# Hybrid encoder block: five weight slots in the down phase, its ring loads on SyncE, weight sums two blocks behind

## The reference

```python
gate, val = jnp.split(u @ w_up[i], 2, axis=-1)
gate = causal_depthwise_conv(gate, ffn_dw_w[i], ffn_dw_b[i])
f = (jax.nn.gelu(gate, approximate=True) * val) @ w_down[i]     # the down phase
h = h + rms_norm(f, g_post_ffn[i])
h = h + (p[i] @ w_ple[i]) * jax.nn.sigmoid(h @ w_ple_gate[i])
```

## Time and profile before

| | us |
|---|---|
| median of three runs | 2694.22 |
| lowest, highest | 2690.03, 2695.8 |
| the profiled execution's own time | 2698.67 |
| its span in the profile | 2696.9 |
| first down phase, 28 blocks | 213.08 |
| second down phase, 28 blocks | 186.04 |

### The profile page before, as it was taken

How to read it: one execution, slowest core, us unless ns; L and a number is a source line. 1 busy time by engine, 2 the same in 40 slices (tenths; PEclk the granted TensorE clock), 3 DMA queues, 4 the chain that set the end, 5 groups by cost and what they waited for, 6 DMA issues and landing times.

```text
span 2696.9 us, 33145 instructions
## 1 busy us (share of the span) xinstructions
PE 2608.7 (97%) x11580; PEld 2126.2 (79%) x11580; DVE 1916.0 (71%) x2607; ACT 823.7 (31%) x1465; POOL 1690.4 (63%) x2012
## 2 busy tenths in 40 slices
PE   9999999999999999999999977999999999979999
PEld 7888888888888887788877755788788888867787
DVE  8975789578957895788887555558777775434376
ACT  2542452345234523333332200013323332300022
POOL 6678233213321331799989854578999998855686
PEclk9999999999999999999999988999999999989999
DMA  8878887878787877356667798647465655777545
GB/s 294 288 260 316 289 300 264 300 273 300 260 299 274 293 270 269 129 204 206 214 224 248 287 335 279 244 146 255 159 210 188 203 186 181 273 290 257 204 138 172
DMA packets 322597, 659.35 MB, mean 244 GB/s; under 512 B 25472, under 2 KB 148608, under 8 KB 313088
## 3 DMA queue, kind: packets, MB, share of 16 engines
q1 hardware_dynamic: 269872, 474.76, 52.2%
q10 hardware_dynamic: 52560, 182.48, 17.7%
HBM read 468.39 MB, written 188.74 MB: 244 GB/s over the span
## 4 chain that ended last, share of the span: by engine, by line
PE 73%; DMA 13%; DVE 6%; POOL 4%; issue 2%; ACT 1%; SPq 1%; ACTq 1%; DVEq 0%
PE ps L1590 8%; PE ps L1584 8%; PE ps L1586 8%; PE ps L1367 6%; PE ps L1353 5%; PE ps L1355 5%; PE ps L1354 5%; PE ps L1363 5%; PE ps L1364 5%; DMA up_quad<-in_quads 5%; DMA sums_kept<-up_quad 4%; PE ps L1421 2%; PE ps L1422 2%; PE ps L1425 2%; PE ps L1702 2%; DMA w_stage<-in_down_raw 2%
## 5 line engine op out<-in xcount | busy, mean ns | idle before, releaser
L786 POOL TENSOR_TENSOR w_lo<-w_stage,w_hi 128x256 fp32r<-128x256 f32 x1280 | 1115.5, 901 | 26.3
L782 POOL CAST w_hi<-w_stage 128x1024 fp32r<-128x1024 f32 (+1 forms) x328 | 379.2, 1156 | 403.8 <-DMA w_stage<-sums_kept 162.1
L1584 PE MATMUL ps<-comb_hi,w_hi 128*128 128x512 f32 x1232 | 480.9, 390 | 7.1 <-ACT first_a L1004 4.2
L1586 PE MATMUL ps<-comb_lo,w_hi 128*128 128x512 f32 x1232 | 479.5, 389 | 0.0
L796 POOL TENSOR_TENSOR up_quad<-up_quad 128x128 f32<-128x128 f32 x100 | 50.5, 505 | 539.8 <-DMA up_quad<-in_quads 539.8
L1590 PE MATMUL ps<-comb_hi,w_lo 128*128 128x512 f32 x1232 | 330.3, 390 | 2.2 <-POOL w_lo L786 2.2
L1954 DVE SCALAR_TENSOR_TENSOR ps<-conv_in,col,ps 128x512 f32<-128x512 f32 x436 | 294.1, 748 | 0.8
L1584 PEld LDWEIGHTS ps<-comb_hi,w_hi 128*128 128x128 f32 x1232 | 231.3, 188 | 60.1 <-ACT first_a L1004 6.5
L1590 PEld LDWEIGHTS ps<-comb_hi,w_lo 128*128 128x128 f32 x1232 | 230.7, 188 | 52.8 <-POOL w_lo L786 5.1
L1586 PEld LDWEIGHTS ps<-comb_lo,w_hi 128*128 128x128 f32 x1232 | 231.3, 188 | 47.7
L1696 PE MATMUL ps<-ring,w_hi 128*128 128x512 f32 x448 | 185.9, 415 | 50.2 <-DVE acc L2333 22.6
(11 more groups left out here) (274 smaller groups left out, 5275.8 us busy)
## 6 DMA issues: line engine op xcount, KB each, us to landing
w_hi<-split_weights SPq DMA_DIRECT2D x138, 512.0 KB, 3.9
w_lo<-split_weights SPq DMA_DIRECT2D x138, 512.0 KB, 5.0
f_kept<-item_parts ACTq DMA_DIRECT2D x136, 512.0 KB, 4.0
w_stage<-sums_kept SPq DMA_DIRECT2D x240, 256.0 KB, 3.4
ring<-f_kept ACTq DMA_DIRECT2D x60, 1024.0 KB, 7.9
w_stage<-in_weights SPq DMA_DIRECT2D x86, 512.0 KB, 4.6
w_stage<-in_up_raw SPq DMA_DIRECT2D x132, 256.0 KB, 3.0
up_quad<-in_quads SPq DMA_DIRECT2D x100, 256.0 KB, 3.2
```

The source lines that it names most:

```text
L782: nc.gpsimd.tensor_copy(w_hi[:, slot, 0:many], w_stage[:, slot, 0:many]).then_inc(w_hi_ready, 1)
L786: last = nc.gpsimd.tensor_tensor(w_lo[:, slot, k:end], w_stage[:, slot, k:end], w_hi[:, slot, k:end].bitcast(F32), ALU.subtract)
L1584: nc.tensor.matmul(ps[:, bank], w_hi[:, slot, first + k], comb_hi[i][:, k], start=start and k == 0, stop=False, skip_group_check=True)
L1586: nc.tensor.matmul(ps[:, bank], w_hi[:, slot, first + k], comb_lo[i][:, k], start=False, stop=False, skip_group_check=True)
```

## The change

- `MORE_SLOTS = 2`: two more weight slots, which lie in the 16 KB that `x_in`, `p_hi_t` and `h_mix` use at other times. Down blocks 3 to 27 of each pair use five slots, the least recently used first; every other block uses three. The slots become separate tensors. A block in a new slot waits at least until the projection's last block is done.
- Ring items 4 to 33 are loaded by SyncE. Items 4 to 11 follow the loads of down blocks 0 to 7. An item from 12 on follows the load of the block five behind the one that frees its buffer (at most block 27), and waits for the freeing block.
- ScalarE's `down_phase` becomes `late_sums`, for the first pair only: it loads two quads at the start, and after block d stores sum d - 2 and loads quad d. VectorE makes sum s after its adds of block s + 2.
- `h_mix` is loaded while blocks 3 to 6 of `down_tile` are issued, once the down phase's last block is done.
- The semaphores `dn_tile` and `dn_half` become one, `dn_product`.

```diff
+MORE_SLOTS = 2
+    _many = SLOTS + (MORE_SLOTS if _b >= B_DN + SLOTS else 0)
+    _slot = min(range(_many), key=lambda i: _used[i])
+    SLOT.append(_slot)
+    PREV.append(max(_used[_slot], PLACE[_c, B_DN] - 1) if _slot >= SLOTS else _used[_slot])
+    _used[_slot] = _n
...
+        for i in range(MORE_SLOTS):
+            w_hi.append(sb(f"w_hi_{SLOTS + i}", [P, 8, P], F32R, at + 8 * i * K))
+            w_lo.append(sb(f"w_lo_{SLOTS + i}", [P, 8, P], F32R, at + (8 * i + 4) * K))
+            w_stage.append(sb(f"w_stage_{SLOTS + i}", [P, 8, P], F32, at + (8 * i + 4) * K))
...
-        RING_AFTER = {1: [7], 2: [8], 3: [9], 4: [10], 5: [11]}
+        RING_AT, RING_FREE = {}, {}
+        for held in range(4, RING):
+            RING_AT[held - 4] = [held]
         for held in range(RING, RINGED):
             group, i = divmod(held - RING, PRODUCTS)
-            RING_AFTER.setdefault((PRODUCTS * (2 * group + 1) + i) // 2, []).append(held)
+            RING_FREE[held] = (PRODUCTS * (2 * group + 1) + i) // 2
+            RING_AT.setdefault(min(RING_FREE[held] + SLOTS + MORE_SLOTS, DNS - 1), []).append(held)
...
+            if x >= RING:
+                engine.wait_ge(block_done, PLACE[a, B_DN + RING_FREE[x]] + 1)
             if 8 <= x < RING:
...
-                slot = n % SLOTS
-                if n >= SLOTS:
-                    sp.wait_ge(block_done, n - SLOTS + 1)
+                slot = SLOT[n]
+                if PREV[n] >= 0:
+                    sp.wait_ge(block_done, PREV[n] + 1)
...
                 if b >= B_DN:
                     at = b - B_DN
+                    for x in RING_AT.get(at, ()):
+                        load_items(sp, a, x)
...
-                    if 1 <= j < 5:
-                        sp.wait_ge(block_done, PLACE[a, B_DN])
-                        load_h_mix(a, j - 1)
+                    if 3 <= j < 7:
+                        sp.wait_ge(block_done, PLACE[a, B_DL])
+                        load_h_mix(a, j - 3)
...
-            def down_phase(a):
-
-                for x in (4, 5, 6):
-                    load_items(act, a, x)
-                if a == 0:
-                    items_stored(act, 0, ITEMS)
-                    load_quads(SUM_STEPS)
-                for d in range(DNS):
-                    done(a, B_DN + d)
-                    for x in RING_AFTER.get(d, ()):
-                        load_items(act, a, x)
-                    if a == 0 and 1 <= d <= LATE_STEPS:
-                        store_sums(SUM_STEPS + d - 1)
-                    if a == 0 and d + 1 < LATE_STEPS:
-                        load_quads(SUM_STEPS + d + 1)
+            def late_sums():
+
+                items_stored(act, 0, ITEMS)
+                load_quads(SUM_STEPS)
+                load_quads(SUM_STEPS + 1)
+                for d in range(2, LATE_STEPS + 2):
+                    done(0, B_DN + d)
+                    store_sums(SUM_STEPS + d - 2)
+                    if d < LATE_STEPS:
+                        load_quads(SUM_STEPS + d)
...
-                        if a == 0 and half and 1 <= step <= LATE_STEPS:
-                            sum_quad(SUM_STEPS + step - 1)
+                        if a == 0 and half and 2 <= step < LATE_STEPS + 2:
+                            sum_quad(SUM_STEPS + step - 2)
```

More of the change, by code:

```diff
@@ L108 @@
     KEPT.append(_kept)
[L109 to L112, removed]
+    _loads[_slot] += 16 if _split and _b < B_UP else 32
+    LOADED.append(_loads[_slot])
+    if _slot < SLOTS:
+        _stores[_slot] += 32 if _kept else 0
+    STORED.append(_stores[_slot] if _slot < SLOTS else 0)
 def block_tiles(b):
@@ L211, in build_kernel @@
         K = 1024
[L212 to L215, removed]
+        w_hi = [sb(f"w_hi_{i}", [P, 8, P], F32R) for i in range(SLOTS)]
+        w_lo, w_stage = [], []
+        for i in range(SLOTS):
+            at = region(4 * K)
+            w_lo.append(sb(f"w_lo_{i}", [P, 8, P], F32R, at))
+            w_stage.append(sb(f"w_stage_{i}", [P, 8, P], F32, at))
         big = region(112 * K)
@@ L463, in build_kernel @@
         x_loaded = [sem(f"x_loaded_{t}") for t in range(TT)]
-        w_loaded = [sem(f"w_loaded_{i}") for i in range(SLOTS)]
+        w_loaded = [sem(f"w_loaded_{i}") for i in range(SLOTS + MORE_SLOTS)]
         w_stored = [sem(f"w_stored_{i}") for i in range(SLOTS)]
@@ L556, in load_quad @@
                 t, i = divmod(at, PRODUCTS)
-                into = w_stage[:, slot, 4 * half:4 * half + 4]
+                into = w_stage[slot][:, 4 * half:4 * half + 4]
                 if i in RAW_PLACE:
@@ L785, in split @@
                     end = min(k + 2, many)
-                    last = nc.gpsimd.tensor_tensor(w_lo[:, slot, k:end], w_stage[:, slot, k:end],
-                                                   w_hi[:, slot, k:end].bitcast(F32), ALU.subtract)
+                    last = nc.gpsimd.tensor_tensor(w_lo[slot][:, k:end], w_stage[slot][:, k:end],
+                                                   w_hi[slot][:, k:end].bitcast(F32), ALU.subtract)
                 last.then_inc(w_lo_ready, 1)
@@ L1348, in ready @@
                 else:
-                    pe.wait_ge(w_loaded[n % SLOTS], LOADED[n])
+                    pe.wait_ge(w_loaded[SLOT[n]], LOADED[n])
             def product(bank, c, b, kk, hi, lo, start, stop):
[L1352 to L1355, removed]
+                slot = SLOT[PLACE[c, b]]
+                nc.tensor.matmul(bank, w_hi[slot][:, kk], hi, start=start, stop=False)
+                nc.tensor.matmul(bank, w_hi[slot][:, kk], lo, start=False, stop=False)
+                return nc.tensor.matmul(bank, w_lo[slot][:, kk], hi, start=False, stop=stop)
             def rounded_there(c, b):
@@ L1417, in by_tile @@
                         ready(c, b + k * n // 8)
-                    slot, first = PLACE[c, b + k * n // 8] % SLOTS, k * n % 8
+                    slot, first = SLOT[PLACE[c, b + k * n // 8]], k * n % 8
                     pe.wait_ge(hi_there, count + k + 1)
                     for o in range(n):
-                        nc.tensor.matmul(ps[:, banks[o]], w_hi[:, slot, first + o], hi[:, k], start=(k == 0), stop=False)
-                        nc.tensor.matmul(ps[:, banks[o]], w_lo[:, slot, first + o], hi[:, k], start=False, stop=False)
+                        nc.tensor.matmul(ps[:, banks[o]], w_hi[slot][:, first + o], hi[:, k], start=(k == 0), stop=False)
+                        nc.tensor.matmul(ps[:, banks[o]], w_lo[slot][:, first + o], hi[:, k], start=False, stop=False)
                     pe.wait_ge(lo_there, count + k + 1)
                     for o in range(n):
-                        last = nc.tensor.matmul(ps[:, banks[o]], w_hi[:, slot, first + o], lo[:, k], start=False,
+                        last = nc.tensor.matmul(ps[:, banks[o]], w_hi[slot][:, first + o], lo[:, k], start=False,
                                                 stop=(k == 7))
@@ L1589, in up_product @@
                 for k in range(H4):
-                    last = nc.tensor.matmul(ps[:, bank], w_lo[:, slot, first + k], comb_hi[i][:, k], start=False,
+                    last = nc.tensor.matmul(ps[:, bank], w_lo[slot][:, first + k], comb_hi[i][:, k], start=False,
                                             stop=stop and k == H4 - 1, skip_group_check=True)
@@ L1686, in down_product @@
                 b = B_DN + at // 2
-                slot, first = PLACE[a, b] % SLOTS, 4 * (at % 2) + o
+                slot, first = SLOT[PLACE[a, b]], 4 * (at % 2) + o
                 x = v // 2 * PRODUCTS + i
@@ L1695, in down_product @@
                 for k in range(2):
-                    nc.tensor.matmul(bank, w_hi[:, slot, first + 2 * k], parts[:, k, 0], start=start and k == 0, stop=False,
+                    nc.tensor.matmul(bank, w_hi[slot][:, first + 2 * k], parts[:, k, 0], start=start and k == 0, stop=False,
                                      skip_group_check=True)
-                    nc.tensor.matmul(bank, w_hi[:, slot, first + 2 * k], parts[:, k, 1], start=False, stop=False,
+                    nc.tensor.matmul(bank, w_hi[slot][:, first + 2 * k], parts[:, k, 1], start=False, stop=False,
                                      skip_group_check=True)
@@ L1701, in down_product @@
                 for k in range(2):
-                    last = nc.tensor.matmul(bank, w_lo[:, slot, first + 2 * k], parts[:, k, 0], start=False,
+                    last = nc.tensor.matmul(bank, w_lo[slot][:, first + 2 * k], parts[:, k, 0], start=False,
                                             stop=stop and k == 1, skip_group_check=True)
-                last.then_inc(dn_tile if o == 0 else block_done if at % 2 else dn_half, 1)
+                last.then_inc(block_done if o and at % 2 else dn_product, 1)
             def down_tile(a, j, s):
```

64 lines of the change are left out of this document (33 added, 31 removed).

## The result

The changed kernel took 2649.72 us in the median of 4 runs (2644.57 to 2651.38), the kernel before 2695.01 us beside it. The ratio is 0.9833 with the 95% interval [0.9814, 0.9851]: 45 us less, a gain clear of the noise. The forecast was 2624 in a range of 2600 to 2656. The profiled execution took 2650.41 us, its span is 2648.6.

A forecast was written before the change was run, and what follows sets the result against it. TensorE is busy nearly throughout, so only its 94.5 us lost in the two down phases could be won. Savings of 42 + 28 = 70 us from 2698.67 gave 2628.7, or 2624 on the median's scale; range 2600 to 2656.

The forecast's parts named there:

- the second rival: Quads stay late: first down phase 196 us, second 162, total 2653; chance 0.17.
- the lead: Down phases: with five slots a weight block is issued 27.2 us ahead, in place of 16.3, less 3.9 for splitting.
- the place in line: Down phases: weights stand in SyncE's queue behind ring loads instead of beside them; block 12 ready at 61.4, due at 65.3.
- no weights under 50 GB/s: Sign that would show the forecast: no weight load under 50 GB/s; the trace before showed 27 GB/s.
- part (4): First down phase, late sums: 11.2 us per turn against 10.9 available; bounds 0 and 10 us, nothing taken beyond Part (3).
- Part (3): First down phase: held by the DMA engines, 171 us, 42 less than before.
- Quads stay late: Rival: ring packets still delay quads, 13 to 14 us per two blocks; phases 196 and 162, total 2653; chance 0.17.
- The prediction's own marks: First phase: DMA share above 0.9 for 100 us, quad waits under 15 us (wrong above 30); second phase near 158.
- All stops go: Rival: sharing one queue ends small packets' waiting; both down phases 154 to 155 us, total 2604; chance 0.20.
- One queue is too narrow: Rival: on SyncE's queue each ring load may pay its whole way to landing; slower, 2751 at 6.0 us each; chance 0.05.
- Nothing changes: Rival: losses move from one wait to another, total 2694; chance 0.03.
- The start: First blocks of each down phase: ring loads ahead of blocks 1 and 2; bounds 0 and 5.2 us, 3 taken.

The follow-up runs named there:

- the kernel with six buffers: The changed kernel with six quad buffers in place of two in the late sums; 2628.43 us, ratio 0.9745.
- the six-buffer pair: Six quad buffers and five slots on the changed kernel: ring loads on SyncE (2628.43 us) against ring loads moved back to ScalarE (2651.01 us).

## Why the prediction was right, and where it was not

**The total: inside the range, in part by luck.** 2649.7 lies within 2600 to 2656, but the forecast's own range ended at 2648; the upper end had been stretched for the second rival. The number is 26 us from the forecast and 3 from that rival's 2653.

**Second phase: right.** It forecast 158 with stops in the first three blocks; 157.4 was measured. Both of its reasons, the lead and the place in line, hold; what it doesn't say is that either alone brings most of it, 21 us by slots and 19.5 by the queue. The mark that it named, no weights under 50 GB/s, is not what cured it: in the changed kernel the median 256 KB load lands after 7.7 to 7.9 us, 33 to 34 GB/s counted from its issue, and with slots alone weights landed later than before.

**First phase: the direction right, the size wrong by 25 us.** The step that failed is part (4): "So sums are hardly late: bounds 0 and 10 us in the phase, and I take nothing beyond (3)". It put a turn at 11.2 us, 3.9 for each transfer, from a lone store's 2.05 us and a packet rate read beside rings. Beside a full queue a transfer took 7.6 to 10.0 us, the long turns over 20, the mean turn 14.6. The rate was not the error: 140 packets in 3 us were measured (last section), 47 per us against its 52. What its 3.9 lacks is that a transfer there waits some 3.5 us for its first packet, where one alone waits 1, and that the next transfer of the same queue stands behind it. The bound of 10 us was too narrow too.

In the same part SyncE's waits for sums were put at 8 to 11 us in two places, at no cost; they were 78.7 us over five, and the ring loads queued behind them then come in bursts. The lateness of the sums is only part of that. With three slots the same waits were 27.6 us, with five slots and the rings and sums as before 79.9: with more slots SyncE waits less for finished blocks and comes to these waits earlier.

**Part (3) describes the kernel with six buffers.** Its 171 us is near what that one takes (173.7, and 171.7 with earlier sums, at shares of 0.94 and 0.96), and the course is right too: block 19 was put at 122 us, PE began it 120.8 us into the phase (counted in the timeline), and demand is light behind. The whole then takes 2628, where 2624 was forecast. It was read as the length of the changed kernel's phase, but that one kept the engines at 0.93 for 102 us and at 0.85 over the whole.

**The rivals.** "Quads stay late" gave 2653 with the phases at 196 and 162, and it had a chance of 0.17. The first phase came out at its length, and with the mean turn of 14.6 us close to its 13 to 14, though it came of turns between 8 and 25; in the second phase the forecast was right. The prediction's own marks say the same: the DMA share was 0.93 over the first 102 us and the second phase fits, but VectorE's wait for quads stayed above 30 us, which it had named as proof against itself. "All stops go" fails at the same place. "One queue is too narrow" is refuted: SyncE's queue carried 45 MB in 157 us. "Nothing changes" is refuted by the 45 us. The start was costed at 3 us plus 2 to 3 for the clock in each phase. In the second it had 3.7 us of waits; in the first it had 6.3 (timeline), and PE began block 3 only 26.6 us into the phase, 10 later than at 5.44 a block.

**Who issues a load.** The Trainium skill, in "DMA: Bandwidth & Descriptors", section "Issuing engines are not separate DMA queues", says that transfers share the same 16 DMA engines whoever starts them, and that issuing from several engines saves only the time of issuing. That fits the first phase's quads, which stayed late when the rings left their queue. By itself it doesn't account for the six-buffer pair, where moving the rings back to ScalarE costs 13 and 8 us. There weights stand beside rings again: the stop of 4.4 us at the second phase's start ends with the cast of a weight whose load took 14.6 us beside rings 4 to 6. Part of the cost can also be when the rings are issued; how much, no run here separates.

## What to carry to other kernels

Count a buffer's whole turn (store, load, operation) at the landing times of the stage in which it runs, not at those of a quiet one, and compare it with the time that its number of buffers gives; shifting the work by a step without another buffer changed nothing here (ratio 0.9995). When loads move to a queue that also waits for results, list what each such wait holds back, the unrelated transfers behind it too, and remember that a deeper prefetch comes to such a wait sooner and stands there longer. An estimate from the DMA engines' busy time is the length of a phase only if nothing in it waits for a single transfer's landing: here two buffers left it 25 us away and six 3.

## What the runs showed of the hardware

A small transfer beside a full queue waits before its first packet. The load of a quad was issued on ScalarE's queue (q10) at 1587.22, when SyncE's queue (q1) was full of rings. In the next 3 us q10 moved no packet; from 1591 to 1594 the queues then moved nearly one for one, as in the earlier trace rows (changed kernel, 1587.3 to 1590.3, then 1591 to 1594):

```profile
q1 hardware_dynamic: 351, 1.26, 105.6%
...
q1 hardware_dynamic: 129, 0.96, 77.8%
q10 hardware_dynamic: 140, 0.26, 23.0%
```

In eight of the ten quad loads that were issued in this phase while SyncE's queue took over 85% of the engines, the first packet came 3.3 to 4.0 us after the issue; where that queue was empty it came after 1.0 us. What the engines do in the 3 us, no run here shows. This load and the store issued behind it landed after 8.6 and 9.2 us, where a lone store takes 2. Cutting the rings' rows to 2 KB left the first packet at 3.4 to 4.1 us in most such loads (counted in that run's trace), and the medians at 5.8 and 6.1 us.

Smaller rows cost the engines more time for the same bytes. In the first phase SyncE's queue moved 47.4 MB in 64.9% of 196.5 us with rings in rows of 8 KB, which is 127.5 us of all 16 engines' packet time, and the same 47.4 MB in 71.4% of 194.0 us, 138.5 us, with rings in rows of 2 KB.

Also, one queue reached a share of 79% of all 16 engines over a whole phase (the second) without being its bound.
